# Seven products for eight in three pairs of down tiles of a two-layer hybrid decoder trunk

## What is computed

```python
def _swiglu(hn, w_gate_up, w_down):
    gu = hn @ w_gate_up
    gate, up = jnp.split(gu, 2, axis=-1)
    return (jax.nn.silu(gate) * up) @ w_down
...
        h = h + _rmsnorm(m, norm_mix_post[l])
        f = _swiglu(_rmsnorm(h, norm_ffn_pre[l]), w_gate_up[l], w_down[l])
        h = h + _rmsnorm(f, norm_ffn_post[l])
```

## Time and profile before

| | us |
|---|---|
| median of 3 runs | 1373.38 (1373.3 to 1374.51) |
| profiled execution, its time | 1372.46 |
| profiled execution, span of the core | 1370.7 |
| PE busy | 1353.5 (99%) |
| DVE busy | 1016.7 (74%) |
| ACT busy | 674.8 (49%) |
| Pool busy | 116.4 (8%) |

### The profile page before, as it was taken

One profiled execution on the slowest core, in us unless ns is written; L12 is line 12 of the kernel. 1 busy time (PEld: TensorE's weight loads), 2 busy tenths in 40 slices (PEclk: granted clock), 3 DMA queues, 4 the chain that ended last, 5 costly groups with the idle time before them and its releaser, 6 DMA issues.

```text
span 1370.7 us, 29093 instructions
## 1 busy us (share of the span) xinstructions
PE 1353.5 (99%) x12134; PEld 1332.7 (97%) x12134; DVE 1016.7 (74%) x1615; ACT 674.8 (49%) x1360; POOL 116.4 (8%) x175
## 2 busy tenths in 40 slices
PE   9999999999999999999999999999999999999997
PEld 8999999999999999999989999999999999999996
DVE  7746796868999888644586468958689989885535
ACT  5235554547545445544542364645575445455543
POOL 0001211000000000022100002110000000000220
PEclk9999999999999999999999999999999999999999
DMA  6332233122333323466413313321222333325773
GB/s 211 109 107 78 67 112 109 47 70 78 101 116 101 116 93 108 136 219 223 162 62 108 109 62 101 108 95 35 82 93 93 114 103 101 115 95 154 221 222 113
DMA packets 70116, 155.91 MB, mean 114 GB/s; under 512 B 20672, under 2 KB 24128, under 8 KB 69984
## 3 DMA queue, kind: packets, MB, share of 16 engines
q1 hardware_dynamic: 59248, 119.36, 26.7%
q0 software_dynamic: 10448, 34.16, 8.2%
q10 hardware_dynamic: 288, 0.52, 0.1%
HBM read 141.16 MB, written 12.85 MB: 112 GB/s over the span
## 4 chain that ended last, share of the span: by engine, by line
PE 90%; DVE 7%; ACT 1%; issue 1%; DMA 0%; DVEq 0%; ACTq 0%; SPq 0%
PE PS L679 51%; PE PS L1234 8%; PE PS L1235 8%; PE PS L1236 8%; PE PS L685 5%; DVE Wl L1887 1%; DVE hT L1925 1%; DVE Xl L1904 1%; DVE mT L1924 1%; PE PS L875 1%; DVE actL L2466 1%; PE PS L859 1%; PE PS L847 1%; PE PS L1021 1%; PE PS L857 1%
## 5 line engine op out<-in xcount | busy, mean ns | idle before, releaser
L679 PE MATMUL PS<-Xh,Wh 128*128 128x260 f32 x1376 | 285.6, 289 | 1.7 <-DVE Wl L1949 1.1
L1302 ACT ACTIVATE Wh<-stage 128x1024 fp32r<-128x1024 f32 x143 | 151.0, 1058 | 265.9 <-PE PS L679 242.0
L679 PE MATMUL PS<-Xh,Wl 128*128 128x260 f32 x1376 | 276.8, 283 | 0.0
L679 PE MATMUL PS<-Xl,Wh 128*128 128x260 f32 x1376 | 276.5, 282 | 0.0
L1887 DVE TENSOR_TENSOR Wl<-stage,Wh 128x1024 fp32r<-128x1024 f32 x143 | 174.6, 1222 | 77.3 <-ACT Wh L1302 76.5
L679 PEld LDWEIGHTS PS<-Xh,Wh 128*128 128x128 f32 x1376 | 211.4, 189 | 5.3 <-DVE Wl L1949 1.8
L679 PEld LDWEIGHTS PS<-Xh,Wl 128*128 128x128 f32 x1376 | 211.8, 188 | 0.0
L679 PEld LDWEIGHTS PS<-Xl,Wh 128*128 128x128 f32 x1376 | 211.8, 188 | 0.0
L1234 PE MATMUL PS<-XU,hiA 128*128 128x260 f32 x448 | 126.8, 283 | 0.0
L1234 PE MATMUL PS<-XU,hiB 128*128 128x260 f32 x448 | 126.8, 283 | 0.0
L1235 PE MATMUL PS<-XU,hiB 128*128 128x260 f32 x448 | 126.6, 283 | 0.0
(11 more groups left out here) (373 smaller groups left out, 2875.1 us busy)
## 6 DMA issues: line engine op xcount, KB each, us to landing
stage<-w_slabs SPq DMA_DIRECT2D x143, 512.0 KB, 3.3
raw<-w_slabs SPq DMA_DIRECT2D x136, 256.0 KB, 2.9
dst<-state_ret POOLq DMA_DIRECT2D x32, 256.0 KB, 3.3
dst<-state_gdn POOLq DMA_DIRECT2D x32, 256.0 KB, 4.7
vb<-v_tmp POOLq DMA_DIRECT2D x32, 256.0 KB, 5.2
out_gdn_sample<-dst POOLq DMA_DIRECT2D x16, 256.0 KB, 3.5
out_ret_sample<-dst POOLq DMA_DIRECT2D x16, 256.0 KB, 3.2
hT<-x_t SPq DMA_DIRECT2D x3, 520.0 KB, 6.5
```

The lines of the kernel that those rows point to most:

```text
L679: ins = mm(pj(slot)[:, a], w[:, ws, pos, :], x[:, a, :], start=first and w is Wh and x is xh, stop=last and w is Wl)
L1302: A(Wh[:, G % NW], stage[:, G % NS], ACT.Copy).then_inc(s["hi_split"], 1)
```

## The change

1. **Weights' order.** The first down tile (0) takes its blocks in the order 0 to 7, 16 to 21, 8 to 15 (`DOWN_FIRST`). Its third slab and that of the last tile are loaded with 6 blocks only.
2. **Seven products.** Tiles 1 to 6 form three pairs. In each, the middle blocks 8 to 15 (a left four and a right four) of the two tiles run as seven products of 4 blocks with three matmuls each, on one column half (`down_products`); the other 14 blocks of both tiles follow plainly into the same banks (`down_rests`). A pair has 8 slabs: `left` and `sums` are loaded (full), `stash` and `last` are not, then come 4 slabs of 7 blocks. DVE makes four weight sums per pair (`down_sums`).
3. **Token sums.** The products' activations are sums of blocks and halves: T1, T2 (space of `hT`), T3, T4 (space of `Xh`). DVE makes them with six instructions per layer (`token_sum`), and ACT and DVE split them (`token_high`, `token_low`). Three sums and one low half are placed at the ends of gate/up steps Q-5 to Q-2, the rest in the first down tile.
4. **Residual.** Because T1 and T2 lie in `hT`, the residual is stored to DRAM in four parts by Pool during the first four Strassen steps, and loaded back in four parts from ACT's queue in the third pair.
5. **Around the products.** Per pair, ACT copies P1 and M5, DVE adds U2, U3 and E; a tile's copy to `fT` becomes two additions of one column half.
6. **State updates.** The units stand at steps 2, 4, 5, 6, 7 of pair 0, steps 2 to 7 of pair 1 and 2 to 6 of pair 2 (`UNITS`); step j of a pair handles slab j + 3 counted from the pair's first, once PE is done with its slab j.

The core of the diff:

```diff
+        UNITS = [(p, j) for p, steps in enumerate(((2, 4, 5, 6, 7), (2, 3, 4, 5, 6, 7), (2, 3, 4, 5, 6))) for j in steps]
...
+                src = w_slabs[l, stored_at(n)].rearrange("p (k n) -> p k n", k=KT)
+                if n >= S_DN and down_kind(n) == "plain" and down_kind(n - 2) == "stash":
+                    sp.wait_ge(s["w_rest"], l * REST + Q * W_STEPS + ((n - S_DN - SIDE) // PER_PAIR + 1) * D_SUMS)
+                elif G >= NS:
                     sp.wait_ge(s["lo_split"], G - NS + 1)
-                sp.dma_start(stage[:, G % NS], w_slabs[l, n if n < S_DN else n + 2 * Q].rearrange("p (k n) -> p k n", k=KT)).then_inc(s[f"slab{G % NS}_loaded"], 16)
+                nb = width(n) if n >= S_DN else KT
+                sp.dma_start(stage[:, G % NS, 0:nb], src[:, 0:nb]).then_inc(s[f"slab{G % NS}_loaded"], 16)
...
+                pool.dma_start(v_tmp[l].rearrange("u o (b e) -> (u o b) e", e=P), vrow[:]).then_inc(s["tmp_stored"], 16)
+                pool.wait_ge(s["h_ready"], nth_norm(l, 2))
+                for i in range(4):
+                    pool.wait_ge(s["p_done"], l * MADE + (i + 1) * UN)
+                    pool.dma_start(h_tmp[l, :, 2 * i:2 * i + 2], hT[:, 2 * i:2 * i + 2]).then_inc(s["tmp_stored"], 16)
...
+                for i, j in enumerate(DOWN_ORDER):
+                    if i % 8 == 0:
+                        wait_slab(l, S_DN + i // 8)
+                    pe.wait_ge(s["act_ready"], l * FT + i + 1)
+                    ins = mm6(0, ring(i // 8), i % 8, actH[:, j], act_low(j), i == 0, i == FT - 1)
+                    if i == FT - 1:
+                        ins.then_inc(s["tile_done"], 1)
+                    elif i % 8 == 7:
+                        ins.then_inc(s["slab_part"], 1)
...
+                    for i, (x, bank, fresh) in enumerate(((b11, 2, True), (b21, 0, True), (t1, 1, True), (t2, 3, True), (b22, 1, False), (t3, 3, False), (t4, 2, True))):
+                        if i % 2 == 0:
+                            wait_slab(l, S_DN + d0 + i // 2)
+                        if p == 0 and x >= t1:
+                            pe.wait_ge(s["xu_rest"], l * X_STEPS + X_SUMS + (T_LO1, T_LO2, T_LO3, T_LO4)[x - t1])
+                        if x == b22:
+                            pe.wait_ge(s["gate_half"], l * GATED + Q * HALVES + p * D_COPIES + D_M5)
+                        elif x == t3:
+                            pe.wait_ge(s["post_done"], l * POSTED + Q * POSTS + p * D_POSTS + D_U2)
+                        elif x == t4:
+                            pe.wait_ge(s["gate_half"], l * GATED + Q * HALVES + p * D_COPIES + D_P1)
+                        for k in range(4):
+                            at_, (xh, xl) = i % 2 * 4 + k, operand(x, k)
+                            mm(PS[:, b0 + bank, 0:HC], Wh[:, ring(d0 + i // 2), at_, :], xh, start=fresh and k == 0, stop=False, skip_group_check=True)
+                            mm(PS[:, b0 + bank, 0:HC], Wh[:, ring(d0 + i // 2), at_, :], xl, start=False, stop=False, skip_group_check=True)
+                            ins = mm(PS[:, b0 + bank, 0:HC], Wl[:, ring(d0 + i // 2), at_, :], xh, start=False, stop=i == 0 and k == 3, skip_group_check=True)
+                        ins.then_inc(s["p_done"], 1)
...
+                for p in range(PAIRS):
+                    down_products(p)
+                    down_rests(p)
...
             def hi(G):
...
+                    if kind == "sums":
+                        act.wait_ge(s["w_rest"], m * REST + Q * W_STEPS + p * D_SUMS + D_S2)
+                        src = Wf[:, G % NW]
...
-                        act_high(8, 2)
+                        act_high(16, 2)
+                        act_high(18, 2)
                         gate_second(q)
-                        act_high(10, 2)
-                        act_high(12, 2)
-                        hi(G0 + S_DN + 2)
-                        for j in range(14, FT - 2, 2):
-                            act_high(j, 2)
                         act_high(FT - 2, 1)
                         act_high(FT - 1, 1)
+                        act_high(8, 2)
+                        hi(G0 + S_DN + 2)
+                        for j in range(10, 16, 2):
+                            act_high(j, 2)
+                        token_high(2)
+                        token_high(3)
...
+                def copy_p1(p):
+                    act.wait_ge(s["p_done"], l * MADE + (Q + p) * UN + 1)
+                    if p:
+                        act.wait_ge(s["tile_free1"], (T0 + T_DN + 2 * p - 1) // 2 + 1)
+                    A(p1, PS[:, down_banks(p).start + 2, 0:HC], ACT.Copy).then_inc(s["gate_half"], 1)
...
+                for i in range(ND - NW):
                     hi(G0 + S_DN + i + NW)
-                    if 3 <= i < 19:
-                        keyed(i - 3)
-                    for k in range(KT - 2):
-                        if (FT * k + FT - 1) // 8 == i:
-                            square_down(k)
-                            if k:
-                                weigh(3, k - 1, fT[:, k - 1])
+                    p, j = divmod(i - SIDE, PER_PAIR)
+                    if j == PER_PAIR - 1 and p + 1 < PAIRS:
+                        copy_p1(p + 1)
+                    if i < SIDE:
+                        continue
+                    if j == 0:
+                        copy_m5(p)
+                        square_down(2 * p)
+                        if p:
+                            weigh(3, 2 * p - 1, fT[:, 2 * p - 1])
+                    elif p + 1 == PAIRS and 3 <= j < 7:
+                        if j == 3:
+                            act.wait_ge(s["p_done"], (l + 1) * MADE)
+                        act.dma_start(hT[:, 2 * j - 6:2 * j - 4], h_tmp[l, :, 2 * j - 6:2 * j - 4]).then_inc(s["x0_loaded"], 16)
+                    if (p, j) in UNITS:
+                        keyed(UNITS.index((p, j)))
+                    if j == 5:
+                        square_down(2 * p + 1)
+                        weigh(3, 2 * p, fT[:, 2 * p])
...
+            def down_sums(l, p):
...
+                a11, a12 = stage[:, G % NS, 0:KT // 2], stage[:, G % NS, KT // 2:KT]
+                a21, a22 = stage[:, (G + 1) % NS, 0:KT // 2], stage[:, (G + 1) % NS, KT // 2:KT]
+                s1, s2 = Wf[:, (G + 1) % NW, 0:KT // 2], Wf[:, (G + 1) % NW, KT // 2:KT]
+                s4, s3 = sf[:, 0:KT // 2], sf[:, KT // 2:KT]
...
+                wait_free(dve, G + 1 - NW)
+                V.tensor_tensor(s1, a21, a22, ALU.add).then_inc(s["w_rest"], 1)
+                dve.wait_ge(s["w_rest"], done + D_S1)
+                V.tensor_tensor(s2, s1, a11, ALU.subtract).then_inc(s["w_rest"], 1)
+                V.tensor_tensor(s3, a11, a21, ALU.subtract).then_inc(s["w_rest"], 1)
+                dve.wait_ge(s["w_rest"], done + D_S2)
+                V.tensor_tensor(s4, a12, s2, ALU.subtract).then_inc(s["w_rest"], 1)
...
                     if k0 == 0:
+                        if n == 3 and a == 0:
+                            dve.wait_ge(s["x0_loaded"], 16 + (l + 1) * 64)
...
+                        if Q - 5 <= q < Q - 2:
+                            token_sum((T_1, T_3, T_2)[q - Q + 5])
+                        elif q == Q - 2:
+                            token_low(0)
...
                 lo(G0 + S_DN + 1)
-                rest_act(8, 2)
+                token_low(1)
+                rest_act(16, 2)
                 post(Q - 1, C21)
-                rest_act(10, 2)
+                rest_act(18, 2)
                 gated(Q - 1)
-                rest_act(12, 2)
-                lo(G0 + S_DN + 2)
-                for j in range(14, FT - 2, 2):
-                    rest_act(j, 2)
                 rest_act(FT - 2, 1)
                 rest_act(FT - 1, 1)
+                for i in (T_3AGAIN, T_21, T_4):
+                    token_sum(i)
+                rest_act(8, 2)
+                lo(G0 + S_DN + 2)
+                for j in range(10, 16, 2):
+                    rest_act(j, 2)
...
+                def down_post(p, n):
...
+                    dve.wait_ge(s["gate_half"], copied + (D_M5 if n == D_E else D_P1))
+                    if n == D_U2:
+                        dve.wait_ge(s["p_done"], made + 4)
+                        ins = V.tensor_tensor(u2, b, p1, ALU.add)
+                    elif n == D_U3:
+                        dve.wait_ge(s["p_done"], made + 6)
+                        if p == 0:
+                            dve.wait_ge(s["tail_stored"], (l + 1) * 16)
+                        ins = V.tensor_tensor(u3, b, p1, ALU.add)
+                    else:
+                        ins = V.tensor_tensor(m5[:], m5[:], p1, ALU.add)
+                    ins.then_inc(s["post_done"], 1)
...
+                for i in range(ND - NW):
+                    p, j = divmod(i - SIDE, PER_PAIR)
+                    if j == 1 and i > SIDE:
+                        down_post(p, D_U2)
+                    elif j == 2 and i > SIDE:
+                        down_post(p, D_U3)
```

(31 more changed lines are left out.)

302 lines of the change are left out of this document (218 added, 84 removed).

## The result

The changed kernel takes 1392.62 us (median of four runs, 1388.24 to 1396.33) against 1373.95 for the kernel before on the same chip: a ratio of 1.0138, 95% interval 1.0126 to 1.0150. So it is slower by 1.4%, some 19 us, where 1389 was forecast.

What follows compares the result with a forecast made beforehand. PE, busy 99%, was taken to bound the kernel; the late state-unit chain, +13.8 us (matmul gain and first-tile waits inside it), and +2 for the residual's return took 1372.46 to 1388.3, median 1389, range 1378 to 1397.

Steps and rivals of the forecast that it cites:

- Removed matmuls: In the down pairs, seven products take 84 matmuls instead of 96; 72 fewer in all at 0.1203 us: -8.7 us.
- The first tile: In the first down tile, PE waits for low halves queued behind new sums on DVE: +3.2 us a layer, +6.4 in all.
- The last gate/up steps and the residual's store: Four added DVE instructions fit the steps' free time and the stores run beside products: 0, up to 0.5 us a layer.
- Copies and sums around the products: Per pair, three PSUM steps and two ACT copies cost 0 if ACT and DVE are free, otherwise counted under state units.
- State units: In the down stage, units fall behind at 5.96 us each, 582.9 to 672.3, delaying the last slabs: +6.9 us a layer.
- The bound of 5.5 a unit: State units on two buffers without any other delay: 11.1 us for two, 5.5 a unit, against 5.1 wanted by the order.
- The residual's way back: Four DMAs on ACT's queue behind the last pair's products, beside the last five units: +1 us a layer, bounds 0 and 6.5.
- The sign named for this: In the down stage, the residual's return stretches state loads over 6 us, which would make the forecast wrong in size.
- The clock: Clock full at 2.4 GHz throughout and PE never off, so the clock adds no term: 0.
- The sum: Whole kernel: 1372.46 + 13.8 for the late chain + 2 for the residual = 1388.3, median 1389 us.
- (c): Rival: DMA saturates, units at 6.3 to 6.5 us, products wait in the second and third pair: 1401 us, chance 0.20.

Runs made afterwards that it cites:

- no_units: The changed kernel without the sixteen state units of each layer (loads, stores and their ACT and DVE instructions left out): 1374.69 us.
- units_early: The changed kernel with the units at steps 1, 2, 4, 5, 6 / 1 to 6 / 2 to 6, none at a pair's step 7: 1392.04 us.
- return_late: The changed kernel with the residual loaded back behind the last unit of each layer, in two DMAs instead of four: 1385.26 us.
- no_return: The changed kernel without the residual's four load-back DMAs; GpSimd writes zeros over hT instead: 1386.29 us.
- ladder: The kernel before with seven PE waits of rising length (1 to 14 GpSimd memsets) put into each layer's gate/up products: 1424.64 us.
- many_short: The kernel before with fourteen PE waits of one length (three memsets each) put into each layer: 1415.53 us.
- low_later: The changed kernel with the low half of T2 moved out of the first tile, behind the first pair's weight sums: 1390.46 us.
- bare: The changed kernel without the sixteen state units of each layer and with the low half of T2 out of the first tile: 1373.36 us.

## Why the prediction was right, and where it was not

**Removed matmuls, -8.7.** Right: PE has 72 fewer, and in no_units the 4.3 us a layer meet 4.0 of waits with their 0.24 each, and the stage is 0.8 us shorter than before's, which has a short wait of its own.

**The first tile, +3.2 a layer.** The mechanism and its size were right, the parts not all. Forecast were 2.6 for blocks 8-9, 0.6 for blocks 10-11 and 0.5 for the third product; measured 2.5, 0 and 0.4. DVE began the three sums at 559.8 (forecast 559.5) and blocks 8-9 at 563.4, and PE found the later blocks ready.

**The last gate/up steps and the residual's store, 0.** Layer 0 comes to its first matmul on actH 0.3 us later. Right within the 0.5 allowed.

**Copies and sums around the products, 0 by themselves.** That a unit in step 7 would stand ahead of M5 was said, and PE waited 3.7 and 2.9 us for it. units_early shows that this is no term of its own: without it the time is the same.

**State units.** Right in kind and near in size: first at 582.06 for 582.9, last at 674.80 for 672.3, 6.18 us apart for 5.96. The bound of 5.5 a unit was found without the return, at 5.50 and 5.73. That the last tile waits behind this chain was seen at PE's row for Wl.

**The residual's way back, +1 a layer.** This term was mis-sized: its worth is 7.4 us in all by return_late and 6.3 by no_return, 3 to 4 a layer with the clock's share, where 1 was taken between 0 and 6.5. The argument "it just fits in the idle quarter" took the average of 30 us of DMA, but the return fell on the last five units' stores and loads, each of which is waited for; where it fell on nothing that is waited for, it was free. The sign named for this, state loads over 6 us, did not show: the three issued behind the return's first DMA landed in 6.0, 4.2 and 5.9 us, and it was the stores in front of them that took 5.3 for 3.0. The Trainium skill, DMA: Bandwidth & Descriptors, section "Issuing engines are not separate DMA queues", cited in the prediction, leaned the right way here: with the DMAs on ACT's queue those on Pool's landed later.

**The clock.** This step was wrong: "PE is never off, so the clock is no term of the sum." It is true of the kernel before and not of one in which PE has begun to wait. In the profiled execution some 9 us (6 x 1.5) go to stretches at 1.2 GHz behind waits of 1.8 us and more. The runs of the changed kernel spread over 8 us where those of before spread over 1.2, and the longer ones have the lower granted clock (1396.33 at 0.990, 1388.24 at 0.994). That the spread is the clock's is not shown: in return_late 1382.71 has 0.993 and 1386.67 has 0.995.

**Layer 1's first quarter, 1.3.** Not seen. It follows from a number that the diff changes, SLABS, through a line that it does not touch.

**The sum.** The chain was to end a layer's products 6.9 us later; it ended them 10.5 later. With 2 for the return the forecast stood at +16 and the median came to +19. That it came so near is in part luck. The terms that were missed or too small, the clock, the return and the 2.5 us ahead of layer 1's down stage, are together far more than 3 us. So the chain of the units was priced too high: in return_late 11.8 us are left over before, 2.5 of them ahead of layer 1's down stage and up to 3 of them the clock's, which leaves some 6 to 9 us for the units and the first tile where 13.8 was forecast. Of the rivals, (c) had something right: PE waits in the third pair, and the last five intervals between units are 6.7 and 6.8 us long on average in the two layers, though all fifteen are 6.18 on average and not its 6.3 to 6.5.

## What to carry to other kernels

A kernel whose PE never waits has a price for the first wait that its own trace can't show: the idle time, a quarter of a microsecond for the pipeline, and for a long one the clock. So an edit that trades matmuls for waits must save clearly more than it makes wait; here 4.3 us of matmuls a layer met 3.7 us of waits, the pipeline's share included, even in the best case. Bytes cost by what they run beside and not by their number: put a bulk transfer behind the last load that somebody waits for. And when a diff changes the count of slots or slabs, look at every expression that takes it modulo a ring.

## What was not expected of the hardware

- Stretches of 3.4 us (or twice that) at 1.2 GHz with single waits of PE of 1.99 to 5.31 us, in all eight cases of the ladder; behind waits of 1.4 us and less there were none in ladder, many_short, low_later or bare. In between it varies: a wait of 1.82 us had one (changed kernel, layer 1), waits of 2.5 us had one in the changed kernel and none in no_units, and one of 2.82 us (units_early) and one of 2.85 (low_later) had none.
- In such a stretch the matmuls are 0.217 us apart for 0.120, so that 3.4 us of it cost 1.5.
- A wait of PE costs 0.24 us more than its idle row shows (1.50 for 1.26).
- DVE instructions with two inputs in SBUF took 3.14 to 3.45 us for 1.22 beside a GpSimd subtraction of two SBUF tiles, and GpSimd's own took 2.98 to 3.25 us for 1,040 columns.
